# 32 of 256 tokens taken out of the dense expert layers and computed from gathered rows on VectorE

## The chip, the cores and the metric

The kernel runs on one core of a Trainium2 chip. The metric is the device time of one launch in microseconds (us). Every number below comes from runs of this kernel and from one profiled execution of it.

## What is computed

A decoder block: two token mixers, a gated merge, and then an expert mixer with product keys. Only the last part is touched. Cut to that part, with the shapes of this case (T = 256 tokens, D = 2048, 8 heads of 16 picks each, 16384 experts):

```python
qp = (xt @ w_q).reshape(T, 8, 128)
s1 = einsum('thd,hnd->thn', qp[..., :64], sub_k1)      # 128 keys
s2 = einsum('thd,hnd->thn', qp[..., 64:], sub_k2)      # 128 keys
v1, i1 = top_k(s1, 16);  v2, i2 = top_k(s2, 16)
vals, flat = top_k(v1[..., :, None] + v2[..., None, :], 16)
experts = e1 * 128 + e2                                # 128 picks for each token
gates = softmax(vals)
hid = gelu(einsum('cd,chkd->chk', xc, u_tab[experts])) # dot products with picked rows of u
out = einsum('chk,chkd->cd', gates * hid, v_tab[experts])
```

`u_tab` and `v_tab` have 16384 rows of 2048 float32 each, 134 MB apiece. The block ends with `x + out` and a last norm.

## The kernel before

One core does everything, in program order on each engine, with semaphores written by hand; no scheduler takes part. All large matrices come as *units* of 1 MB (128 partitions x 2048 float32) from `w_units`, in one running order: 400 units, of which the last 256 are the two expert layers. Unit `n` goes through a pipeline that every stage shares:

- SP loads it into one of two slots of `w_raw` (line 269), as soon as the unit two before it has been read by both ScalarE and VectorE.
- ScalarE rounds it to float32r into one of four slots of `w_hi` (`hi`, line 417). VectorE takes the remainder into `w_lo` (`lo`, line 1158). Both also wait until the unit four before it has been used by TensorE (`unit_done`).
- TensorE multiplies. A product of float32 precision is made of float32r products of upper and lower parts.

The experts are computed densely, for all tokens, and the picks come in as a sparse weight.

**First layer** (`hidden`, one TensorE form, one ScalarE form, one VectorE form; 16 iterations `i` of 8 units `k`). A unit holds 128 rows of u. TensorE makes 16 pairs of matmuls for it: line 1059 (upper part of u, both parts of the 256 tokens side by side, 512 columns) and line 1060 (lower part of u, 256 columns). ScalarE and VectorE sum the two halves into `hs` (lines 682 and 1529), GpSimd multiplies by the norm (`hidden_scale`, line 383), ScalarE applies gelu and stores to `hid_scratch`. Beside it:

- iterations 0 to 7: VectorE runs `route` for 16 groups of 128 tokens x 1 head (top-k, indices, softmax), in four parts between its `lo`s.
- iterations 4 to 13: tables. For each 16 tokens VectorE writes one-hot tiles (`picks_hot`, lines 1488 to 1496), TensorE multiplies them (`table`, line 1086), ScalarE copies the result out (`table_out`, line 647) and stores it to `tab_scratch`. One table an iteration in 4 to 7, two in 8 to 13; 16 in all. The last two iterations have none.

**Second layer** (`experts` on TensorE, `experts_out` on ScalarE and VectorE; 16 iterations of 8 units). A unit holds 128 rows of v as the moving side. The stationary side is `w_up` and `w_low`: 128 experts x 128 tokens of gelu times gate. TensorE makes 24 matmuls of 512 columns for each unit (lines 1110 to 1112), into all eight PSUM banks. Once an iteration GpSimd loads the next 8 units' `h_in` and `g_tab` (`v_load`, lines 376 and 378), and twice an iteration VectorE and ScalarE make `w_up` and `w_low` of four units (`weights`, line 1502, `weights_upper`, line 701, and line 1505).

**End.** For each half of the tokens VectorE adds the sum to `x_nat` (line 1575), ScalarE squares, and line 1581 writes the normed row; SP stores it.

## Time and profile before

| | us |
|---|---|
| median of 3 runs | 2462.76 (2462.08 to 2464.83) |
| the profiled execution, own time | 2464.89 |
| its span, first to last instruction | 2463.2 |
| first expert layer, first to last matmul | 965.1 to 1747.6 |
| second expert layer, first to last matmul | 1747.8 to 2449.7 |

Times in the views are counted from the start of the span. The busy time of a matmul group is a sum of latencies that overlap, so the pace of TensorE is read from the starts of successive matmuls and not from the mean duration. VectorE, ScalarE and GpSimd have strict program order, so a wait there holds back all that stands behind it.

### The profile page before, as it was taken

How to read it: one execution, taken by the hardware profiler on the slowest of the kernel's cores; microseconds unless marked ns; L12 is line 12 of the kernel's file. 1: busy time of each engine (PE TensorE's matmuls, PEld its weight loads, DVE VectorE, ACT ScalarE, POOL GpSimd, SP SyncE). 2: the span in 40 equal slices, each digit the busy share in tenths (PEclk: the TensorE clock that was granted, in tenths of full speed). 3: DMA queues.
4: the chain of work that ended last, by engine and by line, in shares of the span. 5: the costliest groups of instructions: out<-in, count | busy, mean ns of one | idle time of the engine just before them, and what ended most of it. 6: DMA issues, size and time to landing. Idle time of an engine off the chain costs nothing.

```text
span 2463.2 us, 34257 instructions
## 1 busy us (share of the span) xinstructions
PE 2418.7 (98%) x12382; PEld 2054.4 (83%) x12382; DVE 1510.0 (61%) x2035; ACT 1167.4 (47%) x1073; POOL 235.3 (10%) x215
## 2 busy tenths in 40 slices
PE   7999999999999999999999999999999999999997
PEld 6888888788878889888888888888888888888885
DVE  5545766555645555888888767664555545555554
ACT  5534555444544344555556445454443434344342
POOL 0012322000000000111111111111100000000000
PEclk9999999999999999999999999999999999999999
DMA  7755655444465545555556566667667676666662
GB/s 278 270 196 201 214 209 213 148 149 167 140 245 219 217 181 174 208 210 196 205 209 212 220 231 221 226 220 253 251 237 257 243 255 236 235 244 234 244 237 103
DMA packets 84666, 530.18 MB, mean 215 GB/s; under 512 B 9856, under 2 KB 10112, under 8 KB 30448
## 3 DMA queue, kind: packets, MB, share of 16 engines
q1 hardware_dynamic: 58464, 423.65, 48.1%
q0 software_dynamic: 14896, 59.12, 7.0%
q10 hardware_dynamic: 11232, 46.37, 4.7%
q8 instruction: 52, 0.85, 0.1%
q14 instruction: 22, 0.18, 0.0%
HBM read 480.87 MB, written 48.23 MB: 215 GB/s over the span
## 4 chain that ended last, share of the span: by engine, by line
PE 89%; DVE 5%; issue 2%; DMA 2%; ACT 2%; DVEq 0%; ACTq 0%; POOL 0%; SPq 0%; POOLq 0%
PE psum L1059 15%; PE psum L1110 9%; PE psum L1112 9%; PE psum L1111 9%; PE psum L753 9%; PE psum L755 9%; PE psum L754 9%; PE psum L1060 8%; DVE w_lo L1158 2%; PE psum L1086 2%; PE psum L887 1%; DMA w_raw<-in_w_units 1%; ACT w_hi L417 1%; PE psum L1012 1%; PE psum L1013 1%
## 5 line engine op out<-in xcount | busy, mean ns | idle before, releaser
L1158 DVE TENSOR_TENSOR w_lo<-w_raw,w_hi 128x2048 fp32r<-128x2048 f32 x400 | 917.6, 2299 | 642.8 <-ACT w_hi L417 635.0
L417 ACT ACTIVATE w_hi<-w_raw 128x2048 fp32r<-128x2048 f32 x400 | 764.5, 1914 | 775.1 <-DMA w_raw<-in_w_units 643.6
L1059 PE MATMUL psum<-h2T,w_hi 128*128 128x512 f32 x2048 | 720.2, 397 | 0.0
L1060 PE MATMUL psum<-h2T,w_lo 128*128 128x256 f32 x2048 | 573.1, 280 | 0.0
L1059 PEld LDWEIGHTS psum<-h2T,w_hi 128*128 128x128 f32 x2048 | 384.3, 188 | 91.0
L1110 PE MATMUL psum<-w_hi,w_up 128*128 128x512 f32 x1024 | 399.0, 390 | 4.4 <-issue 4.4
L1112 PE MATMUL psum<-w_hi,w_low 128*128 128x512 f32 x1024 | 399.1, 390 | 0.0
L1111 PE MATMUL psum<-w_lo,w_up 128*128 128x512 f32 x1024 | 399.0, 390 | 0.0
L1060 PEld LDWEIGHTS psum<-h2T,w_lo 128*128 128x128 f32 x2048 | 386.5, 189 | 0.0
L753 PE MATMUL psum<-w_hi,hT_hi 128*128 128x512 f32 x768 | 307.0, 400 | 12.8 <-DVE w_lo L1158 12.7
L754 PE MATMUL psum<-w_lo,hT_hi 128*128 128x512 f32 x768 | 300.8, 392 | 0.0
L755 PE MATMUL psum<-w_hi,hT_lo 128*128 128x512 f32 x768 | 300.8, 392 | 0.0
L1110 PEld LDWEIGHTS psum<-w_hi,w_up 128*128 128x128 f32 x1024 | 192.7, 188 | 44.9 <-issue 4.8
L1112 PEld LDWEIGHTS psum<-w_hi,w_low 128*128 128x128 f32 x1024 | 192.6, 188 | 40.0
L1111 PEld LDWEIGHTS psum<-w_lo,w_up 128*128 128x128 f32 x1024 | 192.6, 188 | 39.9
L753 PEld LDWEIGHTS psum<-w_hi,hT_hi 128*128 128x128 f32 x768 | 145.6, 190 | 42.3 <-issue 13.7
L755 PEld LDWEIGHTS psum<-w_hi,hT_lo 128*128 128x128 f32 x768 | 145.2, 189 | 31.3
L383 POOL TENSOR_TENSOR hs<-hs,rs_row 128x512 f32<-128x512 f32 x64 | 100.3, 1567 | 726.1 <-DVE hs L1529 726.1
L754 PEld LDWEIGHTS psum<-w_lo,hT_hi 128*128 128x128 f32 x768 | 145.5, 190 | 28.8
L682 ACT ACTIVATE hs<-psum 128x512 f32<-128x512 f32 x64 | 38.0, 594 | 125.0 <-PE psum L1060 125.0
L701 ACT ACTIVATE w_up<-h_in 128x1024 fp32r<-128x1024 f32 x32 | 33.9, 1061 | 113.3 <-DVE h_in L1502 113.3
L376 POOL DMA_DIRECT2D h_in<-hid_scratch x16 | 11.2, 703 | 580.9 <-DVE w_low L1505 455.4
(302 smaller groups left out, 2328.6 us busy)
## 6 DMA issues: line engine op xcount, KB each, us to landing
w_raw<-in_w_units SPq DMA_DIRECT2D x400, 1024.0 KB, 4.8
hid_scratch<-hst ACTq DMA_DIRECT2D x32, 512.0 KB, 5.9
h_in<-hid_scratch POOLq DMA_DIRECT2D x16, 1024.0 KB, 5.4
g_tab<-tab_scratch POOLq DMA_DIRECT2D x16, 1024.0 KB, 11.5
proj_scratch<-evac ACTq DMA_DIRECT2D x24, 512.0 KB, 4.4
tab_scratch<-gate_a ACTq DMA_DIRECT2D x10, 1024.0 KB, 4.7
tab_scratch<-gate_b ACTq DMA_DIRECT2D x6, 1024.0 KB, 3.9
x_nat<-in_x POOLq DMA_DIRECT2D x2, 2048.0 KB, 8.8
```

The costliest lines, as they stand in the source:

```text
L383: pool.tensor_tensor(both, both, rs_row[:, None, :].to_broadcast([P, 2, S]), ALU.mult).then_inc(hid_scaled, 1)
L417: act.activation(w_hi[:, s % SPLIT, :], w_raw[:, s % RAW, :], ACT.Copy).then_inc(hi_done, 1)
L753: pe.matmul(out, xh[:, kc0 + c, ts], rh, start=st, stop=False, skip_group_check=True)
L754: pe.matmul(out, xh[:, kc0 + c, ts], rl, start=False, stop=False, skip_group_check=True)
L755: ins = pe.matmul(out, xl[:, kc0 + c, ts], rh, start=False, stop=en, skip_group_check=True)
L1059: pe.matmul(psum[:, k % 4, :], uh, h2T[:, c, :, :].rearrange("p a t -> p (a t)"), start=c == 0, stop=False, skip_group_check=True)
L1060: ins = pe.matmul(psum[:, k % 4, S:2 * S], ul, h2T[:, c, 0, :], start=False, stop=c == KC - 1, skip_group_check=True)
L1086: ins = pe.matmul(psum[:, 4 + j // 4, (j % 4) * P:(j % 4 + 1) * P], hots[half][0][:, j, :], hots[half][1][:, j, :], start=True, stop=True, ...
L1110: pe.matmul(out, wh, vh, start=first, stop=False, skip_group_check=True)
L1111: pe.matmul(out, wh, vl, start=False, stop=False, skip_group_check=True)
L1112: ins = pe.matmul(out, wl, vh, start=False, stop=last, skip_group_check=True)
L1158: dve.tensor_tensor(w_lo[:, s % SPLIT, :], w_raw[:, s % RAW, :], w_hi[:, s % SPLIT, :].bitcast(F32), ALU.subtract).then_inc(lo_done, 1)
```

## The change

The first 32 tokens (`G`) are no longer part of the dense layers.

- First layer: the matmuls take 224 tokens (`NU`), so the pair has 448 and 224 columns; `hs`, `hst` and `hid_scratch` shrink alike. The pair count stays.
- Tables: 14 instead of 16. One pair of one-hot tiles and one output tile remain (`hot1a`, `hot2a`, `gate_a`) where there were two. Iterations 8 to 12 have two tables each, 13 has none.
- Second layer: `w_up` and `w_low` keep their shape, with zeros for the first 32 tokens. So TensorE makes the same 24 matmuls for a unit as before.
- The 32 tokens: 32 tokens x 128 picks = 4096 rows of u and 4096 rows of v. They are laid out as four groups of 32 partitions, 32 rows for each partition. Each of 64 indirect transfers brings 128 rows of 8 KB (1 MB) into one of four slots of `ring`. During the first half of the second layer VectorE makes dot products with `hg` (the normed input times the norm's weight, made on GpSimd); then one gelu; during the second half VectorE adds up weighted rows of v in `y_acc`. Four fp32 matmuls with a summing matrix `sel` add the four partition groups into PSUM before the first half's sum is given out.
- The gathers stand on GpSimd's queue, four behind each `v_load`.

The diff, cut to its core:

```diff
+G = 32
+NU = S - G
+NTAB = NU // TB
+RING = 4
+GJ = PICKS * G // P
-I_T1, I_T2, I_T3 = 4, 8, 14
+I_T1, I_T2, I_T3 = 4, 8, 13
@@ gpsimd
+            def gather(n):
+                j = n % GJ
+                rows = io["u_rows"] if n < GJ else io["w_units"].rearrange("a p n -> (a p) n")
+                if n >= RING:
+                    pool.wait_ge(ring_used, n - RING + 1)
+                pool.indirect_dma_start(ring[:, n % RING, :], None, rows,
+                                        bass.IndirectOffsetOnAxis(ap=gidx[:, n // GJ, j:j + 1], axis=0)).then_inc(ring_in[n % RING], 16)
+            pool.wait_ge(x1_done, 4)
+            pool.wait_ge(sc_done, 2)
+            for g in range(P // G):
+                pool.dma_start(x_rep[g * G:(g + 1) * G, :], x_nat[0:G, 0, :]).then_inc(rep_in, 16)
+            pool.wait_ge(rep_in, 16 * (P // G))
+            pool.tensor_tensor(hg[:, :], g2[:, :], x_rep[:, :], ALU.mult).then_inc(hg_done, 1)
...
-            with pool.Fori(1, PEER_NK // (2 * VB)) as i:
-                wait_alone(pool, wlow_done, i * 2)
+            pool.wait_ge(unit_done, V0)
+            pool.wait_ge(gidx_done, 1)
+            for n in range(RING):
+                gather(n)
+            for i in range(1, PEER_NK // (2 * VB)):
+                pool.wait_ge(wlow_done, i * 2)
                 v_load(i)
+                for n in range(4 * i, 4 * i + 4):
+                    gather(n)
@@ scalar
             experts_out(0)
-            with act.Fori(1, PEER_NK // 8 - 1) as i:
+            with act.Fori(1, U_IT // 2) as i:
                 experts_out(i)
+            act.wait_ge(dots_done, 1)
+            act.activation(hid_g[:, :], dots[:, :], ACT.Gelu_apprx_tanh, scale=rs_g[:, 0:1]).then_inc(hidg_done, 1)
+            with act.Fori(U_IT // 2, U_IT - 1) as i:
+                experts_out(i)
@@ tensor
-                        pe.matmul(psum[:, k % 4, :], uh, h2T[:, c, :, :]...)
-                        ins = pe.matmul(psum[:, k % 4, S:2 * S], ul, h2T[:, c, 0, :], ...)
+                        pe.matmul(psum[:, k % 4, 0:2 * NU]..., uh, h2T[:, c, :, G:S], ...)
+                        ins = pe.matmul(psum[:, k % 4, NU:2 * NU], ul, h2T[:, c, 0, G:S], ...)
...
+                if t == 0:
+                    pe.wait_ge(y_done, 1)
+                    pe.wait_ge(sel_done, 2)
+                    for q in range(4):
+                        ins = pe.matmul(psum[:, q, :], sel, y_acc[:, q * NB:(q + 1) * NB], start=False, stop=True, ...)
@@ vector
+            def gathered(n):
+                j, slot = n % GJ, n % RING
+                dve.wait_ge(ring_in[slot], 16 * (n // RING + 1))
...
+                if n == GJ:
+                    dve.wait_ge(hidg_done, 1)
+                    step(dve.tensor_tensor(wts_g[:, :], hid_g[:, :], gsel[:, 2, :], ALU.mult))
+                if n < GJ:
+                    ins = dve.tensor_tensor_reduce(ring[:, slot, :], ring[:, slot, :], hg[:, :], 1.0, 0.0, ALU.mult, ALU.add, dots[:, j:j + 1])
+                    ins.then_inc(ring_used, 1)
...
+                else:
+                    dve.wait_ge(ring_used, n)
+                    dve.scalar_tensor_tensor(y_acc[:, :], ring[:, slot, :], wts_g[:, j:j + 1], y_acc[:, :], ALU.mult, ALU.add).then_inc(ring_used, 1)
...
@@ vector, experts_out(i), at the end of each k
+                    if k % 2 == 1:
+                        gathered(4 * i + k // 2)
```

A new function `gather_rows` (VectorE, iteration 13 of the first layer) makes the row numbers `gidx` from the picks with some fifteen small instructions and clears the first 32 columns of `w_up` and `w_low`.

GpSimd's queue in the second layer. Before, one iteration of its loop, two transfers behind one wait:

```order
L376 ISA [waits w_low_done]
L376 DMA h_in<-hid_scratch 128x2x1024
L378 ISA
L378 DMA g_tab<-tab_scratch 128x16x128
```

Now, from the end of the first layer on; `ring` is the gathers' buffer, `gidx` holds the row numbers:

```order
L405 DMA ring<-in_u_rows,gidx 128x2048 [waits gidx_done,unit_done]
L405 DMA ring<-in_u_rows,gidx 128x2048 x3
L391 DMA h_in<-hid_scratch 128x2x896 [waits w_low_done]
L393 DMA g_tab<-tab_scratch 128x14x128
L405 DMA ring<-in_u_rows,gidx 128x2048 [waits ring_used] x4
```

Four gathers of 1 MB now stand between one `v_load` and the next.

VectorE in the second layer, most of one iteration. Before:

```order
L1158 TENSOR_TENSOR w_lo<-w_raw,w_hi 128x2048 [waits unit_done,hi_done] x4
L1502 TENSOR_TENSOR h_in<-h_in,g_tab 128x1024 [waits v_operands_in,unit_done]
L1505 TENSOR_TENSOR w_low<-h_in,w_up 128x1024 [waits w_up_done]
L1158 TENSOR_TENSOR w_lo<-w_raw,w_hi 128x2048 [waits unit_done,hi_done] x3
```

Now, from the end of one iteration into the next; the row `ring,dots` is a dot product with a gathered tile and the row `dots` gives out its sum:

```order
L1201 TENSOR_TENSOR w_lo<-w_raw,w_hi 128x2048 [waits unit_done,hi_done]
L1572 ISA ring,dots<-ring,g 128x2048 [waits ring_in3]
L1572 ISA dots 128x1
L1201 TENSOR_TENSOR w_lo<-w_raw,w_hi 128x2048 [waits unit_done,hi_done]
L1589 TENSOR_TENSOR h_in<-h_in,g_tab 128x896 [waits unit_done]
L1592 TENSOR_TENSOR w_low<-h_in,w_up 128x4x224 [waits w_up_done]
L1201 TENSOR_TENSOR w_lo<-w_raw,w_hi 128x2048 [waits unit_done,hi_done]
L1572 ISA ring,dots<-ring,g 128x2048 [waits ring_in0]
```

A gathered tile is now read, and waited for, after every second `w_lo`.

TensorE just before the first half of the tokens is given out. In the kernel before, line 1110 follows line 1112 here at once:

```order
L1149 MATMUL psum<-w_hi,w_low 128x512
L1184 MATMUL psum<-y_acc,rs_diag 128x512 [waits sel_done,y_done]
L1184 MATMUL psum<-y_acc,rs_diag 128x512 x3
L1147 MATMUL psum<-w_hi,w_up 128x512
```

Four fp32 matmuls and a wait for VectorE's last weighted sum have been added between the halves.

## Rows read from the trace of the kernel before

**Rows 1.** The page: busy times, and the chain that ended last by engine.

```profile
PE 2418.7 (98%) x12382; PEld 2054.4 (83%) x12382; DVE 1510.0 (61%) x2035; ACT 1167.4 (47%) x1073; POOL 235.3 (10%) x215
...
PE 89%; DVE 5%; issue 2%; DMA 2%; ACT 2%; DVEq 0%; ACTq 0%; POOL 0%; SPq 0%; POOLq 0%
```

**Rows 2.** Timeline of TensorE, first layer, 32 pairs in a row: start, duration, line.

```profile
1602.03 0.39 PE L1059 MATMUL psum<-h2T,w_hi 128*128 128x512 f32 x1
1602.26 0.28 PE L1060 MATMUL psum<-h2T,w_lo 128*128 128x256 f32 x1
...
1612.98 0.40 PE L1059 MATMUL psum<-h2T,w_hi 128*128 128x512 f32 x1
```

**Rows 3.** Timelines of TensorE: 256 columns alone, 64 columns alone, 512 columns alone.

```profile
929.96 0.28 PE L1011 MATMUL psum<-h2T,w_hi 128*128 128x256 f32 x1
...
933.92 0.28 PE L1011 MATMUL psum<-h2T,w_hi 128*128 128x256 f32 x1
...
37.27 7.25 PE L771 MATMUL psum<-w_small,xgT 128*128 128x64 f32 x64
...
1999.82 0.39 PE L1111 MATMUL psum<-w_lo,w_up 128*128 128x512 f32 x1
...
2003.90 0.39 PE L1111 MATMUL psum<-w_lo,w_up 128*128 128x512 f32 x1
```

**Rows 4.** Chain that ended last, first layer: start, length, link.

```profile
1231.43 2.21 DVE w_lo L1158
...
1282.09 2.21 DVE w_lo L1158
...
1391.33 3.57 PE psum L1086 x32
...
1650.21 3.57 PE psum L1086 x32
```

**Rows 5.** Busy by stretch: us, PE, PEld, DVE, ACT, POOL, PE clock, DMA share, GB/s.

```profile
1056.00:1101.00 45.00, 45.00 (x257) 39.02 (x256) 38.84 (x91) 25.73 (x24) 5.47 (x4) 1.00 0.59 208
1245.00:1295.00 50.00, 50.00 (x296) 43.69 (x295) 44.70 (x107) 28.94 (x25) 5.47 (x4) 1.00 0.60 210
1550.00:1600.00 50.00, 50.00 (x308) 44.58 (x308) 34.69 (x48) 26.22 (x18) 7.32 (x4) 1.00 0.61 217
2000.00:2200.00 200.00, 200.00 (x884) 165.64 (x884) 106.04 (x56) 78.43 (x46) 9.35 (x10) 1.00 0.67 242
```

**Rows 6.** Timeline of VectorE, first layer, the same step of two successive iterations.

```profile
1060.44 2.29 DVE L1158 TENSOR_TENSOR w_lo<-w_raw,w_hi 128x2048 fp32r<-128x2048 f32 x1 [0.30 <-ACT w_hi L417]
...
1067.99 0.69 DVE L1529 TENSOR_TENSOR hs<-hs,psum 128x512 f32<-128x512 f32 x1 [0.91 <-ACT hs L682]
...
1105.66 2.29 DVE L1158 TENSOR_TENSOR w_lo<-w_raw,w_hi 128x2048 fp32r<-128x2048 f32 x1 [0.29 <-ACT w_hi L417]
```

**Rows 7.** Transfers in 2000 to 2200 us: queue (packets, MB, share), issues (median us to landing).

```profile
q1 hardware_dynamic: 5229, 38.12, 51.6%
...
w_raw<-in_w_units SPq DMA_DIRECT2D x38, 1024.0 KB, 4.8
```

**Rows 8.** Busy by stretch, as in Rows 5, inside one `v_load` of the second layer.

```profile
2112.00:2117.00 5.00, 5.00 (x23) 4.13 (x22) 0.00 (x0) 0.41 (x1) 0.00 (x0) 1.00 1.02 388
```

**Rows 9.** Timeline of GpSimd, SP and ScalarE around that `v_load`.

```profile
2104.87 0.70 POOL L376 DMA_DIRECT2D h_in<-hid_scratch  x1 [41.21 <-DVE w_low L1505]
...
2107.36 4.82 SPq L269 DMA_DIRECT2D w_raw<-in_w_units  x2
...
2116.59 1.92 ACT L417 ACTIVATE w_hi<-w_raw 128x2048 fp32r<-128x2048 f32 x1 [7.38 <-DMA w_raw<-in_w_units]
...
2118.95 1.92 ACT L417 ACTIVATE w_hi<-w_raw 128x2048 fp32r<-128x2048 f32 x1 [0.45 <-DMA w_raw<-in_w_units]
```

**Rows 10.** Chain that ended last, fp32 matmuls of 256 columns, and the last link.

```profile
939.49 3.46 PE psum L1023 x16
...
2456.54 2.35 DVE out_t L1581
```

More of the change, by code:

```diff
@@ L222, in hybrid_block @@
             "rt_turned", "rt_out", "rt16_done", "hot1_done", "hot2_done", "tab_done", "tab_out")
-        tab_st = sems("tab_stored0", "tab_stored1")
+        tab_st = sem("tab_stored")
+        rep_in, hg_done, gidx_done, dots_done, hidg_done, zero_done, sel_done, y_done = sems(
+            "rep_in", "hg_done", "gidx_done", "dots_done", "hidg_done", "zero_done", "sel_done", "y_done")
+        ring_in = sems(*(f"ring_in{k}" for k in range(RING)))
+        ring_used = sem("ring_used")
         v_in, prod_done, wup_done, wlow_done, acc_done = sems("v_operands_in", "prod_done", "w_up_done", "w_low_done", "acc_done")
@@ L687, in hidden @@
                     if k == 6 and one:
-                        first = isinstance(i, int) and i == I_T1
-                        table_out(i - I_T1, 0, None if first else i - I_T1)
+                        table_out(i - I_T1)
                     if k % 4 == 3 and two:
-                        j, half = i - I_T2, k // 4
-                        first = isinstance(i, int) and i == I_T2
-                        prior = j + (I_T2 - I_T1) if half == 0 else None if first else j
-                        table_out(j * 2 + (I_T2 - I_T1 + half), half, prior)
+                        table_out(i * 2 + (k // 4 - I_T2 - I_T1))
                     if k == 4 and isinstance(i, int) and i == U_IT - 1:
@@ L1064, in hidden @@
                     if k == 5 and one:
-                        table(i - I_T1, 0, 0 if isinstance(i, int) and i == I_T1 else i - I_T1)
+                        table(i - I_T1)
                     if k % 4 == 2 and two:
-                        tb = i * 2 + (k // 4 - I_T2 - I_T1)
-                        table(tb, k // 4, tb)
+                        table(i * 2 + (k // 4 - I_T2 - I_T1))
             def turn_picks(t):
@@ L1077, in turn_picks, with table @@
                 ins.then_inc(rt_turned, 1)
-            def table(tb, half, prior):
+            def table(tb):
                 pe.wait_ge(hot1_done, tb + 1)
                 pe.wait_ge(hot2_done, tb + 1)
-                if not (isinstance(prior, int) and prior == 0):
-                    pe.wait_ge(tab_out, prior)
+                if not (isinstance(tb, int) and tb == 0):
+                    pe.wait_ge(tab_out, tb)
                 for j in range(TB):
-                    ins = pe.matmul(psum[:, 4 + j // 4, (j % 4) * P:(j % 4 + 1) * P], hots[half][0][:, j, :], hots[half][1][:, j, :], start=True, stop=True, skip_group_check=True)
+                    ins = pe.matmul(psum[:, 4 + j // 4, (j % 4) * P:(j % 4 + 1) * P], hot1a[:, j, :], hot2a[:, j, :], start=True, stop=True, skip_group_check=True)
                 ins.then_inc(tab_done, 1)
@@ L1140, in _ @@
                 for k in range(VB, 8):
-                    ins = products(k, t, last=k == 7)
+                    ins = products(k, t, last=t == 1 and k == 7)
+                if t == 0:
+                    pe.wait_ge(y_done, 1)
+                    pe.wait_ge(sel_done, 2)
+                    for q in range(4):
+                        ins = pe.matmul(psum[:, q, :], sel, y_acc[:, q * NB:(q + 1) * NB], start=False, stop=True, skip_group_check=True)
                 ins.then_inc(acc_done, 1)
@@ L1514, in hidden @@
                             dve.wait_ge(rt_out, 1)
-                        picks_hot(i - I_T1, 0, None if first else i - I_T1, [k])
+                        picks_hot(i - I_T1, [k])
                     if k % 4 == 0 and two:
@@ L1520, in hidden @@
                             dve.wait_ge(rt_out, 2)
-                        picks_hot(tb, k // 4, I_T2 - I_T1 if first else tb - 1)
+                        picks_hot(tb)
                     lo(i * 8 + (U0 + k + AHEAD), k + AHEAD)
@@ L1528, in hidden @@
                         both = hs[:, q, :].rearrange("p (a t) -> p a t", a=2)
-                        dve.tensor_tensor(both, both, psum[:, 2 * q:2 * q + 2, 0:S], ALU.add).then_inc(hid_summed, 1)
+                        dve.tensor_tensor(both, both, psum[:, 2 * q:2 * q + 2, 0:NU], ALU.add).then_inc(hid_summed, 1)
+                    if k == 0 and isinstance(i, int) and i == I_T3:
+                        gather_rows()
                     if k == 4 and isinstance(i, int) and i == U_IT - 1:
@@ L1564, in experts_out @@
                         weights(i * 2 + 2, 0)
-            experts_out(0)
-            with dve.Fori(1, PEER_NK // 8 - 1) as i:
-                experts_out(i)
-            experts_out(PEER_NK // 8 - 1, True)
+                    if k % 2 == 1:
+                        gathered(4 * i + k // 2)
+            for i in range(U_IT):
+                experts_out(i, i == U_IT - 1)
             dve.wait_ge(gf_in, 16)
```

105 lines of the change are left out of this document (71 added, 34 removed).

## The prediction, made before the changed kernel ran

> **What bounds the kernel now.** I read the page's busy table and its chain first: TensorE is busy 98% of the span and carries 89% of the chain [rows 1]. So time is won where TensorE's work shrinks, as long as nothing else is close behind it. Two questions follow, one for each layer.
>
> The pace of TensorE comes from the starts in its timeline. In the first layer 31 pairs take 1612.98 - 1602.03 = 10.95 us, 0.353 us for each pair, of which the wide matmul takes about 0.235 and the narrow one 0.118 [rows 2]. Alone, 256 columns take (933.92 - 929.96)/33 = 0.120 us and 512 columns (2003.90 - 1999.82)/18 = 0.227 us, so a column costs 0.417 ns at granted clock 1.00 [rows 3, 5].
>
> Who is close behind? In iterations 0 to 3 of the first layer VectorE is busy 38.84 of 45 us [rows 5]. An iteration there takes 1105.66 - 1060.44 = 45.2 us, and the waits named between these two rows, six of which the longest is shown, add to 2.7 us: VectorE's own sequence needs 42.5 us [rows 6]. In iterations 4 to 7 the one-hot tiles come on top, and the chain runs through `w_lo` with a period of 1282.09 - 1231.43 = 50.7 us [rows 4]: there VectorE, not TensorE, already sets the pace. In iterations 8 to 13 the chain goes from table to table, ten half iterations in 1650.21 - 1391.33 = 258.9 us, 25.9 each, with VectorE at 34.7 of 50 us [rows 4, 5].
>
> In the second layer TensorE's 24 matmuls of 0.227 us for a unit make 43.5 us an iteration; the layer's first and last matmul give 43.9. The weights' transfers have little slack behind that, as worked out below.
>
> **The change, part by part.**
>
> *Pairs of the first layer.* 64 columns fewer save 26.7 ns on the wide matmul. The narrow one goes to 224 columns: 13.3 ns by the slope. But 64 columns alone keep a pace of (7.25 - 0.28)/63 = 0.111 us, far above 64 columns' worth [rows 3], so something other than columns sets a floor, and each of these matmuls has a weight load of its own. I take 0.111 for the narrow one, 7 ns less than now; a pair saves 34 ns, an iteration of 128 pairs 4.35 us. Ends: 26.7 ns (3.4 us), if the present 0.118 is the floor for float32r, and 40 ns (5.1 us) by the slope alone.
>
> The Trainium skill (TensorE: Matmul & The Clock Gate, section LDWEIGHTS) gives a load the time of its columns over 1.2, 107 ns for 128, whatever the matmul's width. It speaks against the narrow matmul's share of the gain; its 107 in place of the row's 111 would save 4 ns more on each of 2048 pairs, 8 us less in the sum if nothing else held.
>
> *By iterations.* 0 to 3: TensorE would need 45.2 - 4.35 = 40.9 us, VectorE 42.5 less four times 0.09 for the smaller `hs`, so VectorE takes over at 42.2: 4 x 2.9 = 11.6 us, ends 8 and 14. 4 to 7: bound by VectorE now; 1 us, ends 0 and 4. 8 to 12: tables stay, 5 x 4.35 = 21.8 us, ends 17 and 25.6; VectorE's 36 us an iteration and ScalarE's less stay covered by 47.4. That one pair of one-hot tiles is left costs nothing as I see it: `picks_hot` stands behind an `hs` sum that already waits for the unit after the table. 13: 4.35 us and two tables; a table is 25.9 - 4 x 5.65 = 3.3 us; 10.9 together. 14 and 15: 8.7. Sum 54 us, ends 42 and 66.
>
> *The beginning.* Copies of `x_nat` and the product `hg` hold GpSimd before its first `hidden_scale`; `hs` of 512 columns takes it 5.47/4 = 1.4 us [rows 5], so 2048 columns some 6 us. Only the stores of hidden rows wait for it, with two iterations to spare. `gather_rows` is small and lies where VectorE has room. Both 0.
>
> *TensorE in the second layer.* Zeros cost as much as numbers: 0 saved.
>
> *Gathers.* 64 MB more in 16 iterations, on engines that are busy 67% of the layer at 242 GB/s [rows 5]. A `w_raw` slot lives through a load of 4.8 us [rows 7], ScalarE's 1.92, VectorE's 2.29 [rows 6, 9] and some 0.4 of issue: 9.4 us, four times an iteration, 37.6 of 43.9. Two slots have 12.5 us to spare. What other traffic does to them shows at a `v_load` of 2 MB: the two loads that SP issues at 2107.36 and 4.8 - 0.3 us later are consumed at 2116.59 and 2118.95, so they took 9.2 and 7.1 us [rows 9], 6.7 more than 4.8 twice, with all engines busy at 388 GB/s [rows 8]. At 14/16 of the bytes that is 5.9 us an iteration, and 6.6 us are left. A gather has half of a `v_load`'s bytes: 3.35 us. If all four lie wholly over loads, they cost 13.4: 6.8 too much on two slots, 3.4 us an iteration, 55 us in all. If they meet loads only in the share of time in which `w_raw`'s bytes flow (51.6% of the engines' time [rows 7]), they cost 6.9, and the excess is nothing. No row shows such a gather, and its descriptors may be slower; I take the middle, 28 us, ends 0 and 55.
>
> The Trainium skill (DMA: Bandwidth & Descriptors, section Specifications) limits HBM to 358 GB/s for a core. Eight units, four gathers and the smaller `v_load` are 14.4 MB in 43.9 us, 329 GB/s, so by the page the layer would run at 92% of the limit. The row above reached 388 and disagrees with the limit; by the row it is 85%.
>
> *VectorE in the second layer.* Four instructions of 2048 elements an iteration; the nearest is line 1581 with 2.35 us [rows 10]: 9.4 us on top of 106.04 x 43.9/200 = 23.3, so 33 of 43.9. Not a bound, but each can stand in front of a `w_lo` that is ready, and what is queued behind a `ring_in` wait is the `w_lo` that frees a slot and feeds TensorE. VectorE runs three units ahead, some 16 us, so single delays vanish. Ends 0 and, if half of every instruction lengthens a slot's round, 4 x 1.2/2 = 2.4 us an iteration, 38 us; I take 0, since the load's 4.8 us leave VectorE free meanwhile.
>
> *Start and middle of the second layer.* Four gathers stand ahead of the first `v_load`: 6 MB on one queue, at 388 GB/s 16 us alone, more when shared, needed after half an iteration, 22 us. 2 us, ends 0 and 6. ScalarE's stop for the gelu once costs a few us in a stream that is three units ahead: 0.
>
> *The end.* Four fp32 matmuls of 512 columns are as many columns as line 1023's eight of 256, 3.46 us [rows 10], and lie on the path: 3.5 us. VectorE's last sum is behind its last `w_lo`, well before TensorE comes there.
>
> *Sum* against the profiled span: 2463.2 - 54 + 28 + 2 + 3.5 = 2442.7. The profiled execution's own time is 2464.9, the median of the runs 2462.8, 0.4 below the span: I forecast **2442 us**.
>
> **Rivals.**
>
> *The gathers hide.* The slots' slack takes them. For: only 6.6 of 12.5 us are left, yet 6.9 are needed by the share of time. Against: two rows of one `v_load` show how strongly loads suffer. Time: 2463.2 - 54 + 2 + 3.5 = 2415.
>
> *The second layer becomes bound by its loads, and the kernel slower.* Each round of a slot lengthens by the whole gather beside it and by VectorE's instructions in front of `w_lo`; a late `v_load` behind four gathers holds VectorE, and with it both slots. Price 55 us by the full overlap and up to 38 more for VectorE; with 10 of those, 65. It decides against the change from (54 - 5.5)/16 = 3.0 us an iteration on. Signs: `w_lo` and `w_raw` in the chain, TensorE below 100% in the second layer. Time: 2463.2 - 54 + 5.5 + 65 = 2480.
>
> *The narrow matmul is slower, not faster.* No float32r matmul of the trace is narrower than 256 columns. If below that it ran at the pace of fp32, 3.46/8 = 0.432 us for 256 columns [rows 10], 224 would take 0.378, and a pair 0.208 + 0.378 = 0.586: 2048 x 0.233 = 477 us more, some 2965 with the rest. Nothing in the trace points to such a step.
>
> **How the numbers follow.** Forecast 0.40, for 2425 to 2457. Gathers hide 0.22, 2405 to 2425. Loads bind 0.31, 2457 to 2500. Narrow matmul 0.04. Another stall, on GpSimd's queue, 0.03. A measurement of this kernel tells some 0.2% (5 us) from no change. Faster are the first two, 0.62; of the third 0.10 lies within 5 us of before, and 0.28 with the last two is slower. The range leaves out the last two and the tips: 2408 to 2492; the likeliest case alone spans 2425 to 2457.
>
> **What would show it.** In the profile after: pairs at 0.319 us (0.313 or 0.326 at the ends); iterations 4 to 7 unchanged near 50.7 us with `w_lo` in the chain; the first layer 54 us shorter, 729 us. In the second layer the load's median above 4.8 us, DMA share near 0.9, TensorE with small gaps, 730 us from 702. If the first layer gives less than 42 us, the pace of pairs or VectorE was misread; if the second keeps 702, the slots' arithmetic was.

## The result, and the profile after

The change makes the kernel a little slower: 2472.0 us, median of 9 runs (8 of them from 2467.84 to 2477.62), against 2464.28 us for the kernel before in the same job (2461.22 to 2467.44); ratio 1.0033, 95% interval 1.0020 to 1.0045. A second job gave 2471.1 against 2466.1, ratio 1.0017 (1.0007 to 1.0027). I forecast 2442 us and a gain. The ninth run took 4751 us, with TensorE's matmuls at about half their usual pace all through, and nothing below rests on it; the profile of after is from the second job.

The page of after, with its busy times and its chain, answers to [rows 1]:

```profile
PE 2363.6 (96%) x12326; PEld 2045.3 (83%) x12326; DVE 1627.9 (66%) x2112; ACT 1145.1 (46%) x1072; POOL 366.0 (15%) x284
...
PE 46%; DVE 18%; DMA 18%; issue 9%; ACT 8%; DVEq 0%; SPq 0%; ACTq 0%; POOL 0%; POOLq 0%
DMA w_raw<-in_w_units 17%; DVE w_lo L1201 10%; PE psum L791 9%; PE psum L793 9%; PE psum L792 9%; ACT w_hi L453 7%; PE psum L1097 6%; PE psum L1098 3%; PE psum L1123 2%; PE psum L925 1%; DVE h_in L1589 1%; DVE hs L1616 1%; DVE y_acc L1581 1%; PE psum L1050 1%; PE psum L1051 1%
```

TensorE lost 55 us of work (2418.7 to 2363.6) and the span still grew by 9.2, from 2463.2 to 2472.4. TensorE carries 46% of the chain instead of 89%: the lines 1147 to 1149, the second layer's products, are no longer among its first links, and the loads of `w_raw`, VectorE's `w_lo` and ScalarE's `w_hi` stand there, 34% together. So the first layer gave what it had, and the second took it back. By the first and the last start on the first matmul line of each layer (1059 and 1110 before, 1097 and 1147 after): first layer 782.5 us before (965.1 to 1747.6), 731.8 after (964.4 to 1696.2); second layer 702.0 before (1747.9 to 2449.9), 762.5 after (1696.6 to 2459.1). That is -50.7 and +60.5.

The second layer in numbers of matmuls. Busy by stretch (us, PE, PEld, DVE, ACT, POOL, PE clock, DMA share, GB/s), the kernel before and then after:

```profile
1760.00:2370.00 610.00, 610.00 (x2693) 505.26 (x2692) 325.60 (x170) 246.08 (x142) 28.08 (x30) 1.00 0.67 244
```

```profile
1760.00:2370.00 610.00, 585.14 (x2526) 477.37 (x2525) 411.75 (x241) 224.95 (x134) 131.69 (x81) 0.99 0.84 311
```

The count says more than the busy column: 167 matmuls fewer in the same 610 us, at 610/2693 = 0.2265 us each, are 37.8 us lost, of which only 24.9 show as idle. Most of the other 12.9 stands in slow matmuls: behind four of the stops the granted clock is at half, for 17 us in all. Behind the one of 2.12 us at 2201.28 nine matmuls run in 3.3 us, in which fourteen have room at the usual pace:

```profile
2201.60:2204.90 3.30, 3.30 (x9) 2.60 (x8) 3.29 (x2) 1.77 (x1) 1.23 (x1) 0.50 0.73 251
```

VectorE is not full (68%), nor are the DMA engines (84%). The rest of the 60.5 us stands at the two ends of the layer. The waits of after in 1720 to 2400 us (total, times, longest):

```profile
ACT w_hi L453 <- DMA w_raw<-in_w_units: 326.9, 86, 11.3
...
DVE w_lo L1201 <- ACT w_hi L453: 191.1, 87, 9.8
...
PEld psum L1147 <- issue: 36.3, 24, 5.6
...
PE psum L1147 <- DVE w_lo L1201: 27.2, 16, 5.3
```

TensorE waits for `w_lo`, VectorE for `w_hi`, ScalarE for the load. One turn of this, in the chain of after:

```profile
2002.61 2.22 DVE w_lo L1201
...
2005.03 10.35 DMA w_raw<-in_w_units
2015.41 1.93 ACT w_hi L453
...
2019.87 6.55 DMA w_raw<-in_w_units
...
2030.90 6.09 DMA w_raw<-in_w_units
...
2047.68 10.37 DMA w_raw<-in_w_units
```

A load of 4.8 us before [rows 7] takes 10.35, then 6.55 and 6.09, then 10.37 in the next iteration. The long one is the load beside a `v_load`; in the kernel before it took 9.2 us there [rows 9]. GpSimd's timeline at the first of them:

```profile
1997.70 0.77 POOL L391 DMA_DIRECT2D h_in<-hid_scratch  x1 [2.61 <-DVE w_low L1592]
1998.45 1.16 POOL L393 DMA_DIRECT2D g_tab<-tab_scratch  x1
2002.88 2.80 POOL L405 DMA_INDIRECT ring<-in_u_rows,gidx  x1 [3.27 <-DVE dots L1572]
2017.25 0.98 POOL L405 DMA_INDIRECT ring<-in_u_rows,gidx  x1 [11.56 <-DVE dots L1572]
```

A gather is issued 4.4 us behind the table load, as soon as VectorE's dot product has freed its slot, and the table load took a median of 11.7 us to land before. Whether this gather is what makes the load longer is tested below.

### The profile page after: what moved, and what is told of

Read it like the earlier page. It is cut to its first block, busy times and chain, and to the rows that moved or that the text cites. A ratio compares the mean times of both kernels' runs of the same rounds, so it can differ in the third digit from the quotient of the medians.

```text
span 4749.7 us, 33973 instructions
## 1 busy us (share of the span) xinstructions
PE 4713.3 (99%) x12326; PEld 3399.6 (72%) x12326; DVE 1631.0 (34%) x2112; ACT 1151.1 (24%) x1072; POOL 277.2 (6%) x284
## 3 DMA queue, kind: packets, MB, share of 16 engines
q1 hardware_dynamic: 58464, 423.65, 24.9%
## 4 chain that ended last, share of the span: by engine, by line
PE 99%; DVE 0%; ACT 0%; issue 0%; DMA 0%; ACTq 0%; DVEq 0%
PE psum L1097 17%; PE psum L791 11%; PE psum L793 11%; PE psum L792 11%; PE psum L1147 10%; PE psum L1149 10%; PE psum L1148 10%; PE psum L1098 9%; PE psum L1123 2%; PE psum L925 1%; PE psum L1050 1%; PE psum L886 1%; PE psum L1051 1%; PE psum L1049 1%; PE psum L847 1%; PE psum L957 0%
## 5 line engine op out<-in xcount | busy, mean ns | idle before, releaser
L1097 PE MATMUL psum<-h2T,w_hi 128*128 128x448 f32 x2048 | 1203.8, 611 | 0.0
L1098 PE MATMUL psum<-h2T,w_lo 128*128 128x224 f32 x2048 | 847.0, 414 | 0.0
L1097 PEld LDWEIGHTS psum<-h2T,w_hi 128*128 128x128 f32 x2048 | 629.6, 307 | 172.8 <-issue 143.7
L1147 PE MATMUL psum<-w_hi,w_up 128*128 128x512 f32 x1024 | 691.3, 675 | 4.4 <-issue 4.4
L1149 PE MATMUL psum<-w_hi,w_low 128*128 128x512 f32 x1024 | 690.5, 674 | 0.0
L1148 PE MATMUL psum<-w_lo,w_up 128*128 128x512 f32 x1024 | 690.3, 674 | 0.0
L1098 PEld LDWEIGHTS psum<-h2T,w_lo 128*128 128x128 f32 x2048 | 649.4, 317 | 0.0
L791 PE MATMUL psum<-w_hi,hT_hi 128*128 128x512 f32 x768 | 527.3, 687 | 12.6 <-DVE w_lo L1201 12.6
L792 PE MATMUL psum<-w_lo,hT_hi 128*128 128x512 f32 x768 | 518.1, 675 | 0.0
L793 PE MATMUL psum<-w_hi,hT_lo 128*128 128x512 f32 x768 | 517.9, 674 | 0.0
```

What stands on the lines that cost most here:

```text
L791: pe.matmul(out, xh[:, kc0 + c, ts], rh, start=st, stop=False, skip_group_check=True)
L792: pe.matmul(out, xh[:, kc0 + c, ts], rl, start=False, stop=False, skip_group_check=True)
L793: ins = pe.matmul(out, xl[:, kc0 + c, ts], rh, start=False, stop=en, skip_group_check=True)
L1097: pe.matmul(psum[:, k % 4, 0:2 * NU].rearrange("p (a t) -> p a t", a=2), uh, h2T[:, c, :, G:S], start=c == 0, stop=False, skip_group_check ...
L1098: ins = pe.matmul(psum[:, k % 4, NU:2 * NU], ul, h2T[:, c, 0, G:S], start=False, stop=c == KC - 1, skip_group_check=True)
L1147: pe.matmul(out, wh, vh, start=first, stop=False, skip_group_check=True)
```

## The experiments

Theory after the result: **the weights' loads bind the second layer**, as the second rival had it, because the gathers use up the slots' spare time and more. Open were: transfers or VectorE, total bytes or place, and what the ends of the layer cost. Times of kernels below are medians, of 4 runs where no other number is given; stops, stretches and layers are read from one traced execution of each. The kernel before had 2466.1 to 2466.6 us in these three jobs.

### The change again, and its two halves

`again` is the changed kernel once more (10 runs).

> The changed kernel as it is, for a trace at its usual pace. If the prediction's first-layer term holds, the first expert layer takes 729 us (783 before) and the second has taken the gain back: 702 + some 55 to 60 us. If instead VectorE and the clock cost more in the first layer than I saw, the first layer takes 745 us or more and the second under 740.

`dense_only` has no gathers and none of their work on VectorE and ScalarE:

```diff
-                for n in range(4 * i, 4 * i + 4):
-                    gather(n)
...
             def gathered(n):
...
                 if n == GJ:
...
                     dve.wait_ge(tab_st, 16 * NTAB)
...
+                    dve.memset(y_acc[:, :], 0.0).then_inc(y_done, 1)
```

> Leaves out the contribution of the 32 tokens: no gathers, no dot products, no weighted sums, no gelu for them (y_acc is set to zero). Everything else is the changed kernel. Theory A (the second layer pays for the gathers): 2463 - 54 + 3.5 = about 2413, second layer 702. Theory B (the first layer gives little): over 2435, with the first layer at 750 or more.

`traffic_only` (10 runs) has all gathers, and VectorE only waits for each and frees its slot:

```diff
             def gathered(n):
+                slot = n % RING
                 dve.wait_ge(ring_in[slot], 16 * (n // RING + 1))
...
+                dve.sem_inc(ring_used, 1)
```

> Leaves out VectorE's and ScalarE's work on the gathered rows; all 64 gathers are made, and VectorE waits for each and frees its slot at once. If it is traffic in front of the weights' loads that costs the time, this run is as slow as the changed kernel (within 10 us). If VectorE's 64 instructions in front of w_lo cost it, this run is near dense_only.

`vector_only` has VectorE's 64 instructions and no gathers (the ring holds zeros):

```diff
-                dve.wait_ge(ring_in[slot], 16 * (n // RING + 1))
+                dve.wait_ge(ring_in[slot], 1)
...
-                for n in range(4 * i, 4 * i + 4):
-                    gather(n)
```

> Leaves out the 64 gathers: the ring is set to zero once and VectorE makes its 64 instructions on it, with ScalarE's gelu and all order kept. If VectorE's instructions cost the time, this is as slow as the changed kernel; by the traffic theory it is within 5 us of dense_only.

Measured: again 2471.1 us; dense_only 2426.9 (ratio 0.9837, 0.9820 to 0.9854); traffic_only 2471.3 (1.0021, 1.0011 to 1.0030); vector_only 2446.0 (0.9909, 0.9888 to 0.9930). Over dense_only the gathers cost 44.4 us, VectorE's work 19.0 by itself, and the two together 44.2. They do not add. I read it so that who waits for a load that is late anyway loses nothing by an instruction in front of `w_lo`. The transfers alone make the whole loss. Of the 19.0, some 6 arise ahead of the second layer, where the two kernels do the same work: in vector_only's traced execution it starts at 1702.9 instead of 1696.6; the layer itself is 13.2 us longer.

Two expectations failed here. vector_only was to lie within 5 us of dense_only and lies 19.0 above. And dense_only was to take 2413 us with a second layer of 702: it took 2426.9, and its second layer takes 715.0. Without a single gather, its first iteration takes 52.5 us, every other one 43.5. This has its place in the account below. Busy by stretch of dense_only, vector_only and traffic_only:

```profile
1760.00:2370.00 610.00, 610.00 (x2693) 505.28 (x2692) 319.41 (x170) 240.72 (x142) 24.62 (x28) 1.00 0.66 235
```

```profile
1760.00:2370.00 610.00, 605.32 (x2666) 499.61 (x2665) 428.70 (x252) 236.04 (x140) 25.31 (x28) 1.00 0.66 231
```

```profile
1760.00:2370.00 610.00, 586.74 (x2534) 480.53 (x2533) 301.07 (x162) 226.42 (x133) 153.48 (x81) 0.98 0.83 313
```

dense_only keeps the 2693 matmuls of before to the last one; traffic_only loses 159 (36.0 us).

### How many gathers, and which

Three kernels take traffic_only and keep 16, 32 or 48 of its gathers (the rest of the 32 tokens' work is left out as there): `first_only` those with `n % RING == 0`, which go out right behind a `v_load`; `odd_only` those with odd `n`; `not_first` all but the first kind.

```diff
                 for n in range(4 * i, 4 * i + 4):
-                    gather(n)
+                    if n % RING == 0:
+                        gather(n)
```

> traffic_only with 16 of its 64 gathers: only those with n % 4 == 0, which are the ones that go out right behind the loads of hidden values and tables; the 32 tokens' rows are otherwise neither fetched nor used (their part of the result is left out). dense_only was 2426.9 and traffic_only 2471.3, a difference of 44.4 us. Theory A (collision with these loads): these 16 alone cost most of it, 25 to 44 us: 2452 to 2471 us. Theory B (bytes, in proportion): a quarter of it, 11 us: 2438 us. Rival D (threshold: nothing is lost until the spare time of both buffers is used up): under 3 us, 2427 to 2430 us.

> traffic_only with 48 of its 64 gathers: all but those with n % 4 == 0, so that the gather right behind the loads of hidden values and tables is missing and the rest stands where it stood; the 32 tokens' part of the result is left out. Theory A (collision): little is left, 0 to 15 us over dense_only: 2427 to 2442 us. Theory B (bytes, in proportion): three quarters of 44.4, 33 us: 2460 us. Rival D (threshold): between, 2435 to 2455 us.

> traffic_only with 32 of its 64 gathers, those with n % 2 == 1, two in each iteration and none of them right behind the loads of hidden values and tables; the 32 tokens' part of the result is left out. Over dense_only's 2426.9 us one gather an iteration cost 2.3 us (first_only), three 17.9 (not_first), four 44.4 (traffic_only). Threshold theory (the gathers first use up the 123 us that ScalarE stands waiting for TensorE in dense_only, some 8 us an iteration, and only what is above that costs): two an iteration cost 0 to 6 us, 2427 to 2433 us, and ScalarE's wait for TensorE is near zero or small. Rival (in proportion to the count): 22 us, 2449 us.

| gathers an iteration | kernel | us (lowest to highest) | over dense_only | second layer, traced | stop at its end | matmuls lost in 1760 to 2370 |
|---|---|---|---|---|---|---|
| 0 | dense_only | 2426.9 (2424.7 to 2427.4) | 0 | 715.0 | 4.43 | 0 |
| 1, behind `v_load` | first_only | 2429.2 (2423.8 to 2432.4) | 2.3 | 722.7 | 7.27 | 45 |
| 2, elsewhere | odd_only | 2431.5 (2422.8 to 2436.5) | 4.6 | 726.0 | 10.64 | 24 |
| 3, elsewhere | not_first | 2444.8 (2438.9 to 2447.6) | 17.9 | 731.9 | 7.67 | 60 |
| 4 | traffic_only | 2471.3 (2469.3 to 2476.5) | 44.4 | 759.5 | 10.96 | 159 |

The cost is not a share of the bytes. 16 and 48 gathers cost 2.3 and 17.9 us apart, and 44.4 together; by the traced layers 7.7 and 16.9, and 44.5. What one and two gathers cost lies within the spread of these runs, and their traced executions were the slowest of the four. My collision theory asked for 25 to 44 us in first_only and is wrong in that form; the threshold is what the table shows. Whether the place counts beside the number, it does not show: one gather behind a `v_load` loses 45 matmuls and two elsewhere 24, but half of the 45 go with one stop of 3.64 us, at 1778.21, and from 1790 on the two kernels lose 22 and 24. Where the spare time is, ScalarE's waits in 1720 to 2400 us tell, in dense_only and in first_only:

```profile
ACT w_hi L449 <- DMA w_raw<-in_w_units: 178.3, 58, 9.9
ACT w_hi L449 <- PE psum L1143: 123.3, 47, 8.4
```

```profile
ACT w_hi L455 <- DMA w_raw<-in_w_units: 308.3, 103, 12.6
...
ACT w_hi L455 <- PE psum L1149: 0.7, 1, 0.7
```

A wait for TensorE means that a load was early. There are 123 us of it with no gather and 0.7 with sixteen: these turn spare time into waiting at a small price. The second still costs little; the third and the fourth are paid.

### Where in the iteration a gather goes out

`hold_gathers` (6 runs) is the changed kernel with one line more: GpSimd waits for its `v_load` before the next gather.

```diff
                 v_load(i)
+                pool.wait_ge(v_in, 32 * (i + 1))
                 for n in range(4 * i, 4 * i + 4):
                     gather(n)
```

> The changed kernel with one wait more: GpSimd holds the first gather of each iteration until the two loads of hidden values and tables (1.8 MB, landed 5 to 6 us after issue) have landed; bytes, gathers and VectorE's work are the same. In the trace of the changed kernel the first gather goes out 4.4 us behind the table load (2002.88 behind 1998.45) and ScalarE then waits 9.3 us for a weight load, four times as long as for the others. Theory A (collision: a weight load, the two loads and a gather in flight at once): the wait shrinks to the 7.4 us of before, TensorE's stalls go for the most part, 2440 to 2455 us. Theory B (bytes: the 64 MB of gathers take their share of the transfers wherever they are put): 2468 to 2474 us, the same as the changed kernel's 2471. Rival C: the held gather comes late to VectorE and its work falls behind: above 2475 us, with waits of VectorE for ring.

`spaced_gathers` holds the last gather of an iteration behind the `v_load` too:

```diff
                 v_load(i)
-                for n in range(4 * i, 4 * i + 4):
+                pool.wait_ge(v_in, 32 * (i + 1))
+                for n in range(max(RING, 4 * i - 1), 4 * i + 3):
+                    if n == 4 * i:
+                        pool.wait_ge(unit_done, V0 + 8 * (i - 1) + 4)
                     gather(n)
+            gather(2 * GJ - 1)
```

> hold_gathers (2458.9 us) with the order shifted by one gather: the last gather of an iteration, which in the changed kernel goes out 4.8 us ahead of the loads of hidden values and tables, is held behind them too, and the next one until TensorE has done half of the iteration's units. Bytes and VectorE's work are the same. Collision theory: what keeps gathers away from these loads on both sides gives more than keeping them away on one: 2446 to 2456 us. Bytes theory: hold_gathers has taken what there is to take, the DMA engines stay at 0.86 of their time: 2457 to 2461 us. Rival C (a held gather comes late and VectorE waits): above 2461 us.

Measured: hold_gathers 2458.9 us (ratio to before 0.9965, 0.9952 to 0.9978), spaced_gathers 2494.3 (1.0129, 1.0092 to 1.0167). Same bytes, same instructions on VectorE, and 35 us apart, with the changed kernel's 2471 between them. GpSimd's timeline, hold_gathers and then spaced_gathers:

```profile
1993.57 1.16 POOL L393 DMA_DIRECT2D g_tab<-tab_scratch  x1
2005.50 1.00 POOL L405 DMA_INDIRECT ring<-in_u_rows,gidx  x1 [10.76 <-DMA g_tab<-tab_scratch]
2011.98 2.80 POOL L405 DMA_INDIRECT ring<-in_u_rows,gidx  x1 [5.48 <-DVE dots L1573]
2022.51 2.75 POOL L405 DMA_INDIRECT ring<-in_u_rows,gidx  x1 [7.74 <-DVE dots L1573]
```

```profile
2006.79 1.16 POOL L393 DMA_DIRECT2D g_tab<-tab_scratch  x1
2019.35 1.00 POOL L405 DMA_INDIRECT ring<-in_u_rows,gidx  x1 [11.41 <-DMA g_tab<-tab_scratch]
2020.66 0.98 POOL L405 DMA_INDIRECT ring<-in_u_rows,gidx  x1 [0.30 <-issue]
2025.46 2.74 POOL L405 DMA_INDIRECT ring<-in_u_rows,gidx  x1 [3.82 <-DVE dots L1576]
```

hold_gathers ended between its two theories (2440 to 2455 and 2468 to 2474 us), and the sign that I had named did not come: the wait for the load beside the `v_load` was to shrink to the 7.4 us of before. ScalarE's wait there, in after and in hold_gathers:

```profile
2010.53 1.92 ACT L453 ACTIVATE w_hi<-w_raw 128x2048 fp32r<-128x2048 f32 x1 [9.28 <-DMA w_raw<-in_w_units]
```

```profile
2005.26 1.92 ACT L454 ACTIVATE w_hi<-w_raw 128x2048 fp32r<-128x2048 f32 x1 [8.84 <-DMA w_raw<-in_w_units]
```

Over all iterations the longest wait within 16 us of a `v_load` has a median of 9.1 us in after and 9.0 in hold_gathers, though there no gather follows the `v_load` for 12 us. The waits within these 16 us add to 158 and 162, the others fell from 169 to 128 us. So the 12 us don't come from keeping a gather off the `v_load`. In hold_gathers the gathers are 6.5 to 10.5 us apart. In spaced_gathers three of them, 3 MB, go out within 6.1 us: the wait for half of the units had passed before the `v_load` had landed, so it spaced nothing, and I had built a burst. The expectation was wrong by 40 us; VectorE never waits for a gathered tile there, the sign of rival C, so I put the number down to the bunching. That is argued: the order changed with it, and whether the gather ahead of a `v_load` is worth moving stays open. Stretches of hold_gathers and spaced_gathers:

```profile
1760.00:2370.00 610.00, 594.00 (x2592) 487.35 (x2591) 417.71 (x246) 230.52 (x137) 144.81 (x82) 0.99 0.86 319
```

```profile
1760.00:2370.00 610.00, 574.49 (x2456) 466.19 (x2455) 397.70 (x234) 218.76 (x129) 108.52 (x77) 0.98 0.82 301
```

Of the 167 matmuls 66 came back in the one (15 us), and 70 more were lost in the other. The DMA engines are busier where the kernel is faster: a mean share of 0.82 to 0.86 is not the bound.

### The stop at the end

TensorE waits once for all four last units before the last products. The idle time before line 1147 in TensorE's timeline of after, and at the same place (line 1110) before:

```profile
2432.19 0.77 PE L1147 MATMUL psum<-w_hi,w_up 128*128 128x512 f32 x1 [13.59 <-issue]
```

```profile
2427.15 0.47 PE L1110 MATMUL psum<-w_hi,w_up 128*128 128x512 f32 x1 [4.43 <-issue]
```

`tail_units` (10 runs) waits for each unit by itself and puts unit 4's products for tile 1 behind those for tile 0; `before_tail_units` (10 runs) does the same in the kernel before.

```diff
-            pe.wait_ge(hi_done, UNITS)
-            pe.wait_ge(lo_done, UNITS)
             for t in range(NT):
-                for k in range(VB, 8):
+                for k in range(VB + t, 8):
+                    if t == 0:
+                        pe.wait_ge(hi_done, UNITS - 8 + k + 1)
+                        pe.wait_ge(lo_done, UNITS - 8 + k + 1)
                     ins = products(k, t, last=t == 1 and k == 7)
+                    if t == 0 and k == VB:
+                        products(k, 1)
```

> The changed kernel with the wait for all four last weight units before TensorE's last 97 products split up: each unit waited for by itself in tile 0's products, and unit 4's products of tile 1 put behind its products of tile 0. The trace of the changed kernel has TensorE idle for 13.6 us there, from 2418.6 to 2432.2, while units 4, 5 and 6 were ready by 2418.0, 2422.5 and 2427.6. Theory (the joint wait makes the stop): four blocks of 2.6 us fit in before the last unit is ready, so 9 to 13 us less than the changed kernel's 2471: 2458 to 2462 us, with the stop at most 3 us a piece. Rival (the last loads and the last step of VectorE set the end whatever the order): less than 4 us, 2467 to 2471 us.

> The kernel before with the split of the wait for the last four units alone, as in tail_units. The kernel before stands still for 4.43 us there, its units ready earlier. If the joint wait is the reason for it: 3 to 5 us less than the kernel before. Rival (tile 0 now ends only 7.8 us ahead of tile 1 rather than 10.4, and its last steps delay tile 1's): 0 to 2 us less.

Measured: tail_units 2461.2 us (ratio 0.9976, 0.9963 to 0.9990), 9.9 less than the changed kernel. TensorE's timeline there has three short stops, 4.2 us together, in place of the one of 13.59:

```profile
2428.26 0.47 PE L1147 MATMUL psum<-w_hi,w_up 128*128 128x512 f32 x1 [0.86 <-DVE w_lo L1204]
2432.87 0.47 PE L1147 MATMUL psum<-w_hi,w_up 128*128 128x512 f32 x1 [1.64 <-DVE w_lo L1204]
2437.55 3.70 PE L1187 MATMUL psum<-y_acc,rs_diag 128*128 128x512 f32 x8 [1.70 <-DVEq L1587]
```

before_tail_units gave 2459.4 against 2466.4 (0.9970, 0.9959 to 0.9981), 7.0 less for a stop of 4.43 us. I had expected 3 to 5. The traces show 6.2 of it in the second layer, which takes 696.2 us from its first to its last matmul where it took 702.4: the stop, and some 1.8 us that the nine matmuls behind it lost at half clock (told in the last section). So the edit is worth something without the change, and whatever is built from the change is to be held against 2459, not against 2466.

### All three together

`all_three` is hold_gathers, tail_units, and a mended start of the second layer. There TensorE's first tile 0 products wait for the last hidden sum (3.03 us in after, 6.7 in dense_only, none before); ScalarE's copy for it stands behind a `w_hi`.

```diff
-                    hi(i * 8 + (U0 + k + AHEAD), k + AHEAD)
+                    last = isinstance(i, int) and i == U_IT - 1 and k == 7
+                    if not last:
+                        hi(i * 8 + (U0 + k + AHEAD), k + AHEAD)
...
+                    if last:
+                        hi(i * 8 + (U0 + k + AHEAD), k + AHEAD)
```

VectorE's `lo` moves in the same way behind its `hs` sum.

> hold_gathers and tail_units together, and at the start of the second layer ScalarE's copy and VectorE's sum of the last hidden unit put ahead of the split of the weight unit that comes in three units later (TensorE waited 5 to 7 us there for that sum). If the three stops are separate: hold_gathers 12.2 us, tail_units 9.9 us, the entry 4 to 6 us, so 2471 less 26 to 28: 2443 to 2446 us, under the kernel before (2466.6) by 0.9%. If they share their cause, since a stop gives the weight loads time to catch up: 2448 to 2458 us.

Measured: 2445.3 us (2441.1 to 2452.0, 4 runs; 0.9922, 0.9893 to 0.9951), 26 less than the changed kernel. That fits gains that add (12.2 + 9.9 + 4 to 6), but four runs over 11 us do not shut out the 2448 to 2458 of the other theory. The start's stop is 0.16 us, yet the layer's first iteration still takes 48.7 us, with another stop at its end, for a late `w_lo`:

```profile
1698.82 0.50 PE L1152 MATMUL psum<-w_hi,w_up 128*128 128x512 f32 x1 [0.16 <-DVE hs L1626]
...
1744.39 0.54 PE L1152 MATMUL psum<-w_hi,w_up 128*128 128x512 f32 x1 [3.95 <-DVE w_lo L1209]
```

Busy by stretch of all_three:

```profile
1760.00:2370.00 610.00, 594.65 (x2602) 488.23 (x2601) 420.28 (x245) 230.01 (x136) 139.57 (x82) 1.00 0.87 321
```

It is faster than the kernel before by 21 us, and than before_tail_units, run in the same job, by 14. It still loses 91 matmuls (20.6 us) between 1760 and 2370, and ScalarE still waits 286.6 us for loads. Without that loss it would stand near 2425 us. That this is dense_only's time too is chance: dense_only still has its stops at both ends of the layer.

## Why the prediction was wrong

Against the forecast of 2442.7 for the span, 29.7 us are missing. By the traces 3.3 of them lie in the first layer, 7.5 in what the second layer costs without any gather (5.5 forecast, 13.0 in dense_only), 16.4 in the gathers (28 forecast, 44.4), and the rest, 2.5, mostly in VectorE's work beside them (3.1 by the traced layers, nothing by the medians). The time itself lies inside the range that I gave; the sign is wrong.

**The first layer's sum was near, by luck in part.** 54 us forecast, 50.7 measured. Pairs in after:

```profile
1559.82 0.37 PE L1097 MATMUL psum<-h2T,w_hi 128*128 128x448 f32 x1
1560.03 0.26 PE L1098 MATMUL psum<-h2T,w_lo 128*128 128x224 f32 x1
1560.13 0.37 PE L1097 MATMUL psum<-h2T,w_hi 128*128 128x448 f32 x1
```

From 1559.82 the thirteenth next pair starts at 1563.89: 0.313 us a pair, the end that I had for the slope alone, 0.319 forecast. The floor of 0.111 us that I took from 64-column matmuls isn't there at 224 columns, where narrow to next wide is 0.102 on the mean of the first five; the 64-column rows were of fp32 matmuls, 64 records for 32 matmuls, and not of the float32r form that I priced with them. The Trainium skill (TensorE: Matmul & The Clock Gate, section LDWEIGHTS) has 107 ns for a weight load of 128 columns; the trace lies 5 ns below it and can't tell whether the load or the columns set the 0.102. The narrow-matmul rival is out. By iterations (every 128th start on the first matmul line): 0 to 3 took 181.1 us and take 165.6, 15.4 less where I had 11.6. The first two run at TensorE's pace, 40.3 and 40.1 us (40.9 forecast), the next two near VectorE's, 42.2 and 43.1 (42.2 forecast, with waits of 2.7 us where the six of [rows 6] add to 2.6). But 4 to 7 took 201.6 us and take 209.6: 8.0 us lost where I had 1 won. TensorE now stops there for the one-hot tiles, 21.7 us where it was 4.5:

```profile
1247.60 2.28 DVE w_lo L1201
...
1298.78 2.29 DVE w_lo L1201
```

```profile
PE psum L1123 <- DVE hot2a L1537: 21.7, 4, 5.5
```

The period is 51.2 us, 50.7 before [rows 4]: bound by VectorE, as forecast. What TensorE had won ahead of it is handed back there in good part: 0 to 7 together gave 7.5 us and not 12.6. Iterations 8 to 13 gave 34.6 (32.7 forecast), the last two 8.5 (8.7). From 8 on, tables stand 23.63 us apart (nine half iterations from 1355.18 to 1567.82) where they stood 25.9 apart:

```profile
1355.18 3.58 PE psum L1123 x32
...
1567.82 3.58 PE psum L1123 x32
```

That is 2.27 us a half iteration; I had 2.2.

**The failed step is the price of the gathers.** The sum had 28 us for them, ends 0 and 55; traffic_only over dense_only is 44.4. The working gave about 6.6 us an iteration left for two slots, and up to 3.35 us for each gather. dense_only shows the spare time (123 us of ScalarE's waits in 680 us, which are 15.2 iterations of 44.7, 8.1 each), and the table shows that two gathers nearly fit and the third and fourth are paid. What failed is the overlap. I set full overlap against overlap in proportion to `w_raw`'s share of the engines' time, 51.6%, by which the excess was nothing, and went halfway between, for no reason of its own. But that is the share of the engines' time that the bytes fill, not the share of time in which a load can be delayed. From issue to landing of each load, at least one is under way in 83% of 1760 to 2370 us in the kernel before, in 85% in dense_only and 93% in odd_only. An estimate with 0.83 in the same working: four gathers lie over loads for 13.4 x 0.83 = 11.1 us, 4.5 more than the 6.6, 2.3 on two slots, 36 us in all. Measured are 44.4, of which 6.5 are the stop at the end: 38 in the layer, 2.4 an iteration, where whole overlap gives 3.4. For three gathers the estimate is 14 (17.9 measured), for two nothing (4.6). That the excess over the slots' spare time is what is paid is argued from this agreement; no run changed the number of slots.

**A place was missing: the end.** I priced the fp32 matmuls (3.5; measured 3.43) and not the joint wait for the four last units, though [rows 1] has the issue share in which it hides. It grew from 4.43 to 13.59 us, as the last unit is there later and TensorE has run up to it. It takes no gather for that: vector_only has 11.44. In dense_only it is 4.43, in traffic_only 10.96, so some 6.5 of the gathers' 44.4 us are this stop. tail_units shows it: 9.9 us.

**The start** was 2 in the sum, for a late `v_load`. Measured, the second layer's first iteration takes 51.1 us where it took 43.6: a stop of 3.03 us for the last `hs` sum, one of 2.44 at 1747.68 for a `w_lo`, and 3.4 us at half clock behind each. In dense_only, without gathers, it takes 52.5. Neither the size nor the reason was right. all_three shows that the last `hs` sum waits behind the splitting of a later weight unit; why that costs time here and not before, no run took apart.

**VectorE** was 0 in the sum and is 0 beside the gathers (2471.1 against 2471.3). By itself it is 19.0: vector_only's stop at the end is 11.44 us, and 27 matmuls (6.1 us) are lost in the middle. My reason, that VectorE is free while a load runs, was wrong; beside the gathers it is hidden by a larger loss, and may come back when the loads are mended.

**The rivals.** The second was right in its mechanism, its signs (`w_raw` and `w_lo` in the chain, TensorE under 100%) and nearly its time: 2480 for 2472, though its full 55 us for the gathers and 10 for VectorE were 44.4 and none. Its decision point, 3.0 us an iteration, compares with 60.5 - 3.4 = 57.1 us, 3.6 an iteration, that the second layer really lost. The gathers do not hide. I gave 0.31 to it and 0.40 to a value between that no mechanism stood behind.

**The sum, remade with what was measured:** 2463.2 - 50.7 + 37.8 (1760 to 2370) + 9.2 (growth of the end's stop) + 3.4 (fp32) + 3.0 (start) = 2465.9. Left to the span of 2472.4 are 6.5 us, and nearly all of it is the start once more: the stop of 2.44 us at 1747.68 and two stretches of 3.4 us at half clock, 1.6 lost in each.

## What to carry to other kernels

- When a stream of loads has spare time, write down the spare time for each round and the whole price of one added transfer. For the overlap, the share of time in which a load is under way (here 0.83) came near the measured price, the share that its bytes fill (0.52) did not; full overlap is the safe one. An average share of busy DMA engines (here 0.82 in the slowest and 0.87 in the fastest kernel with all 64 gathers) says nothing on it.
- The order and spacing of added transfers count as well as their number: with the same bytes one wait on GpSimd's queue gave 12 us, and a kernel with a burst of three cost 23.
- Look at each joint wait (for the last of several producers) on the path. It is small while the consumer is the slowest and grows by itself when a producer becomes so.

## What the runs showed of the hardware

A stop of TensorE can cost more than its length. After the 13.59 us stop the granted clock is at half, and the busy row of the next 3.5 us reads:

```profile
2432.00:2435.50 3.50, 3.31 (x8) 2.67 (x9) 3.40 (x3) 0.00 (x0) 0.00 (x0) 0.50 0.00 0
```

From 2432.75 to 2437.02 ten matmuls start 0.427 us apart where 0.227 is the pace at clock 1.00, so this stop cost 2 us more. After the 4.43 us stop of before the row from 2427.0 has 0.58. In tail_units, whose stops there are 0.86 to 1.70 us long, the clock from 2418 to 2445 is 1.00. Between these the length alone does not tell: after the 2.12 us stop at 2201.28 in after the clock is at half, after the one of 2.43 us at 1874.37 it is 1.00.

An indirect transfer of 128 rows of 8 KB (1 MB) landed a median of 9.5 us after its issue in traffic_only, and its instruction held GpSimd for 0.94 to 3.05 us. With all 64 of them the engines reach 321 GB/s over 610 us (all_three). The Trainium skill (DMA: Bandwidth & Descriptors, section Specifications) has 358 GB/s as the limit of a core; no stretch of 610 us here passes it, and the one of 5 us in [rows 8] did with 388.
